# Output projection of the last token tile split between the attention steps and the tail, and a new order inside each attention step, in a two-block transformer kernel

## What is computed

```
# block 1, layers 0 and 1
mod = silu(c) @ w_ada[layer] + b_ada[layer];  shift, scale, gate = split(mod)
h = rmsnorm(x, g_pre) * (1 + scale) + shift
z = h @ w_in
layer 0: o = concat(mla_attention(8 heads), sliding_window_attention(8 heads))
layer 1: o = concat(rmsnorm((softmax(q1 k1) - lam * softmax(q2 k2)) @ v),   # 4 heads, "dif"
                    forgetting_attention(8 heads))                            # "fox"
y = (o * silu(z_gate)) @ w_out
x = x + gate * rmsnorm(y, g_post)
# block 2, layer 2
h = x @ w_in; o = concat(nsa(6 heads) * silu, stick_breaking(4 heads) * silu, hgrn2(6 heads) * silu)
x = layer_norm(ALPHA * x + o @ w_out)
```

## Time and profile before

| | |
|---|---|
| median of 3 runs (lowest, highest) | 1437.36 us (1437.13, 1442.88) |
| profiled execution | 1442.61 us |
| its span in the trace, mean granted clock | 1441.1 us, 0.926 |
| PE busy | 1264.0 us, 88% |
| DVE, ACT, POOL busy | 554.3, 427.3, 113.7 us |

### The profile page before, as it was taken

One profiled execution on the slowest core, in us unless ns is written; L12 is line 12 of the kernel. 1 busy time (PEld: TensorE's weight loads), 2 busy tenths in 40 slices (PEclk: granted clock), 3 DMA queues, 4 the chain that ended last, 5 costly groups with the idle time before them and its releaser, 6 DMA issues.

```text
span 1441.1 us, 15111 instructions
## 1 busy us (share of the span) xinstructions
PE 1264.0 (88%) x5264; PEld 699.6 (49%) x5264; DVE 554.3 (38%) x1422; ACT 427.3 (30%) x1086; POOL 113.7 (8%) x140
## 2 busy tenths in 40 slices
PE   4889986899998999889999989989998999856974
PEld 1555543445564444334455555555454545545541
DVE  3233322333544520334442432112125731667871
ACT  0133022334432201322234332114233533651211
POOL 0000000000001000000000000000000000484722
PEclk9989997999998999999999999989999999966986
DMA  9222334444000432322111004241101111000000
GB/s 349 92 81 64 112 117 172 146 175 118 1 1 1 117 59 59 52 67 58 59 59 59 1 11 131 59 161 44 45 0 45 44 59 59 1 0 31 1 30 29
DMA packets 60258, 99.71 MB, mean 69 GB/s; under 512 B 12068, under 2 KB 22129, under 8 KB 60184
## 3 DMA queue, kind: packets, MB, share of 16 engines
q1 hardware_dynamic: 54370, 93.58, 20.8%
q10 hardware_dynamic: 5814, 5.18, 1.1%
HBM read 96.60 MB, written 4.08 MB: 70 GB/s over the span
## 4 chain that ended last, share of the span: by engine, by line
PE 72%; DVE 14%; ACT 5%; issue 3%; DMA 3%; POOL 2%; ACTq 1%; DVEq 0%; SPq 0%; POOLq 0%
PE PR L856 29%; PE SC L908 6%; PE OB L886 6%; PE PT L768 6%; PE PR L768 4%; PE OB L768 4%; PE SC L768 4%; PE PT L923 3%; PE PR L949 3%; DMA ring<-in_w_ada 3%; DVE d L1661 2%; DVE stage L1661 2%; POOL arena L1569 2%; DVE tok L1661 1%; DVE arena L1877 1%
## 5 line engine op out<-in xcount | busy, mean ns | idle before, releaser
L856 PE MATMUL PR<-ring,hT 128*128 128x512 f32 (+1 forms) x784 | 381.2, 599 | 9.3 <-DVE arena L1817 6.3
L1349 ACT ACTIVATE stage<-stage,nmax 128x256 f32<-128x256 f32 (+7 forms) x200 | 103.7, 519 | 335.3 <-DVE nmax L1981 311.2
L856 PEld LDWEIGHTS PR<-ring,hT 128*128 128x128 f32 x784 | 136.3, 198 | 114.4 <-issue 98.4
L886 PEld LDWEIGHTS OB<-arena,pts 128*128 128x128 f32 (+3 forms) x880 | 132.2, 202 | 97.4 <-issue 75.9
L908 PE MATMUL SC<-arena 64*128 64x256 f32 (+15 forms) x432 | 147.5, 452 | 10.0 <-DVE nmax L1981 10.0
L856 PE MATMUL PR<-hT,ring 128*128 128x512 f32 (+1 forms) x304 | 152.8, 626 | 0.0
L1569 POOL TENSOR_TENSOR arena<-arena 128x192 f32<-128x192 f32 (+1 forms) x118 | 80.5, 683 | 826.1 <-PE OB L886 778.2
L886 PE MATMUL OB<-arena,pts 128*128 128x64 f32 (+4 forms) x880 | 131.0, 278 | 9.2 <-ACT pts L1197 9.2
L923 PEld LDWEIGHTS PT<-ident,stage 128*128 128x128 f32 (+3 forms) x440 | 58.2, 145 | 131.0 <-issue 65.1
L923 PE MATMUL PT<-ident,stage 128*128 128x128 f32 (+3 forms) x440 | 87.5, 290 | 34.7 <-ACT stage L1328 15.9
L1197 ACT ACTIVATE pts<-PT 128x256 f32<-128x256 f32 (+7 forms) x200 | 80.7, 404 | 58.4 <-issue 22.2
(11 more groups left out here) (337 smaller groups left out, 1306.6 us busy)
## 6 DMA issues: line engine op xcount, KB each, us to landing
ring<-in_w_ada SPq DMA_DIRECT2D x12, 2048.0 KB, 8.8
ring<-in_od_w_in SPq DMA_DIRECT2D x8, 2048.0 KB, 14.6
ring<-in_w_in SPq DMA_DIRECT2D x5, 1536.0 KB, 6.8
ring<-in_ev_w_in SPq DMA_DIRECT2D x3, 2048.0 KB, 7.7
ring<-in_w_in SPq DMA_DIRECT2D x3, 2048.0 KB, 9.8
ring<-in_ev_w_out SPq DMA_DIRECT2D x2, 2048.0 KB, 10.1
ring<-in_od_w_out SPq DMA_DIRECT2D x2, 2048.0 KB, 8.7
ring<-in_w_out SPq DMA_DIRECT2D x2, 2048.0 KB, 7.8
```

Source lines behind the costliest of these rows:

```text
L856: mm = pe.matmul(dst, l, r, start=(k == 0), stop=(k == KT - 1))
L886: mm = pe.matmul(ob[:, h * w:h * w + w], pts[0:rows_, v % 2, n * P:n * P + P], vb, start=(n == 0), stop=(n == len(blocks) - 1))
L1349: give(act.activation(pb[:, s % NP, 0:n], zm[:, s % 2, 0:n], ACT.Exp, bias=nmax[:, row, c:c + 1], scale=-1.0, accum_out=rsum[:, row, c:c + ...
```

## The change

1. **Output projection ahead.** Of the last tile's output projection in layers 0 and 1 (16 calls: two halves h of 8 calls over k), the 4 calls of each half whose k belongs to the first half of the mixed features become filler at the end of the attention ("ahead", 4 units each), and so does the transpose `mT` that they need. Their two groups stay open in the two filler banks; `last_tile` transposes the other half and closes them with the other 4 calls each.
2. **`SPREAD`.** To fit this, the spread of layers 0 and 1 is new. In layer 1, 14 steps carry the first 15 tiles in place of 15 steps (8 or 9 units each in place of 8).
3. **Order in a step, all layers.** DVE: `finish_gates`, weights of v, masks of the new scores, and then `finish_behind`, which does for the step **before** the late group part, the group, the chains and `tile_done` of all tiles but `mT` and `hT` ("urgent", still in their own step). ACT: exponentials, `finish_behind` of the step before, copy of the transposed weights, urgent tiles.

```diff
+AHEAD = {0: 0, 1: 0}
+def last_ahead(L):
+    return [("mT", L, T - 1, AHEAD[L])], [("ahead", L, 0), ("ahead", L, 1)]
...
-SPREAD = [[(4, 5)] + [(3, 4)] * 6 + [(5, 9), (2, 1), (4, 10), (2, 1), (2, 9), (2, 5)], [(15, 15), (4, 12), (4, 8), (2, 1), (2, 5), (2, 1), (2, 1), (2, 5)], [(21, 68), (4, 14)]]
+SPREAD = [[(4, 5)] + [(3, 4)] * 6 + [(5, 9), (2, 1), (4, 10), (2, 1), (2, 7), (2, 1), (1, 1), (2, 5)], [(15, 14), (4, 11), (1, 1), (2, 1), (2, 7), (2, 1), (2, 6), (2, 1), (2, 1), (4, 5)], [(21, 68), (4, 14)]]
...
-UNITS = {"adac": 1, "adas": 2, "adag": 1, "mT": 1, "hT": 1}
+UNITS = {"ahead": 4, "adac": 1, "adas": 2, "adag": 1, "mT": 1, "hT": 1}
+URGENT = ("mT", "hT")
+def urgent(done):
+    return [name for name in done if name[0] in URGENT]
...
+            def output_half(L, h, g):
+                i = T - 1
+                p = prn["y", L, i, h]
+                if g == AHEAD[L]:
+                    b = free_bank(p)
...
+                freed(pe, ("mT", L, i, g))
+                W = weights(("wo", L, h))
+                for k in range(4 * g, 4 * g + 4):
+                    mm = pe.matmul(b[:, :], hT[:, k, i * P:i * P + P], W[:, k, :], start=(k == 4 * AHEAD[L]),
+                                   stop=(k == 7 - 4 * AHEAD[L]))
...
+                behind = None
                 for r_, (v, (_, g, j, sus), new) in enumerate(steps(L)):
+                    done = schedule[L][1][r_] if r_ < len(schedule[L][1]) else []
+                    finish_gates()
+                    if r_:
+                        finish_weights(v, g, sus)
                     for s in new:
...
+                    if behind:
+                        finish_behind(*behind)
+                    if urgent(done):
+                        finish_gates()
+                    for name in urgent(done):
+                        tile_done(name)
+                    behind = (v, done)
+                finish_gates()
+                finish_behind(*behind)
                 finish_group(L, len(plan[L]) - 1)
```

More of the change, by code:

```diff
@@ L194, in last_tile @@
     def last_tile(L):
-        jobs.extend(finish_tile(L, T - 1))
+        jobs.append(("mT", L, T - 1, 1 - AHEAD[L]))
+        jobs.extend(("y", L, T - 1, h) for h in range(2))
         chunk_end[("wo", L, 0)] = chunk_end[("wo", L, 1)] = len(jobs)
@@ L202, in fillers @@
         for name, tiles in FILLERS[L]:
-            chunk(name, tiles)
+            chunk(name, [t for t in tiles if t[0] != "ahead"])
     jobs.append(("cols",))
@@ L327, in two_block_kernel @@
     beside |= {("gate0", 0, 0), ("gate1", 0, 0), ("gate1", 0, 1), ("nz", 0)}
+    beside |= {("y", L, T - 1, h) for L in (0, 1) for h in range(2)}
+    late_halves = {("mT", L, T - 1, 1 - AHEAD[L]) for L in (0, 1)}
     bank_of, nth, per_bank, turn = [], [], [0] * 8, [0, 0]
@@ L807, in tile_matmuls @@
                     L, i, g = name[1:]
-                    if kind == "mT" and g == 0:
+                    if kind == "mT" and i == T - 1:
+                        ahead, last = (2 * i, 2 * i + 1) if L == 0 else (i, T + i)
+                        pe.wait_ge(ob_free, g_no[L, ahead if g == AHEAD[L] else last] + 1)
+                    elif kind == "mT" and g == 0:
                         pe.wait_ge(ob_free, g_no[L, 2 * i + 1 if L == 0 else T + i] + 1)
@@ L814, in tile_matmuls @@
                     yield
+                    return
+                if kind == "ahead":
+                    yield from output_half(*name[1:], AHEAD[name[1]])
                     return
@@ L959, in last_tile @@
                     pe.wait_ge(pt_ev[r], (sum(e[0] <= L for e in v_units) + 1 - r) // 2)
-                for name in finish_tile(L, T - 1):
-                    whole_tile(name)
+                late = 1 - AHEAD[L]
+                whole_tile(("mT", L, T - 1, late))
+                for h in range(2):
+                    for _ in output_half(L, h, late):
+                        pass
                 for i in LEFT[L]:
@@ L1328, in stick_tail, with finish_behind @@
                         give(act.activation(pb[:, s % NP, 0:n], zm[:, s % 2, 0:n], ACT.Exp), p_done, s + 1)
+                def finish_behind(r_, v, done):
+                    if v >= 1 and v_units[v - 1][0] == L and last_v[L, v_units[v - 1][1]] == v - 1 \
+                            and v_units[v - 1][3][0][0] == "dif":
+                        rsqrt(DH)
+                    for chain in chains:
+                        next(chain, None)
+                    for name in done:
+                        if name[0] not in URGENT:
+                            tile_done(name)
+                        if name[0] == "hf":
+                            next(chains[-1])
+                    if L == 2 and r_ in HG_EARLY:
+                        exponentials(HG_EARLY.index(r_))
+                behind = None
                 for r_, (v, (_, g, j, sus), new) in enumerate(steps(L)):
+                    done = schedule[L][1][r_] if r_ < len(schedule[L][1]) else []
                     for s in new:
@@ L1362, in attention @@
                     give(copy(pts[0:r, v % 2, 0:w], PT[v % 2][0:r, 0:w]), pt_ev[v % 2], v // 2 + 1)
[L1363 to L1374, removed]
+                    for name in urgent(done):
+                        tile_done(name)
+                    behind = (r_, v, done)
+                finish_behind(*behind)
             def exponentials(c):
@@ L1985, in attention @@
                         stick_tail()
[L1986 to L2009, removed]
+                    if r_ == 0:
+                        finish_weights(v, g, sus)
+                    if behind:
+                        finish_behind(*behind)
+                    if urgent(done):
+                        finish_gates()
+                    for name in urgent(done):
+                        tile_done(name)
+                    behind = (v, done)
+                finish_gates()
+                finish_behind(*behind)
                 finish_group(L, len(plan[L]) - 1)
```

49 lines of the change are left out of this document (45 added, 4 removed).

## The result

The changed kernel takes 1497.32 us (median of 4 runs, 1494.61 to 1501.32) against 1440.12 us for the kernel before: a ratio of 1.0396, 95% interval 1.0352 to 1.044. It is slower by 57 us. I had forecast slower by 17, with a range that ended at 1467.

The account below looks back on a forecast made before the run. PE was taken to bound the kernel, busy for 1264.0 of 1441.1 us. Terms summed to +17.4 on the profiled 1442.61, 1460.0, or 1455 us against the runs' median of 1437.36; range 1430 to 1467, likeliest 1445 to 1466.

Parts of the forecast that it names:

- the first mechanism, the late releases: All layers: filler bank releases stand behind the next step's masks, so PE waits; likeliest case, 1445 to 1466 us, chance 0.67.
- the sum: Whole kernel: 14 + 2 + 12 + 4.8 - 9.5 - 5.4 - 0.5 = +17.4 us.
- Waits of the banks: Layer 0 gates and layer 1 dif steps: PE waits for late filler bank releases, about 40 us in all.
- Dif steps: Layer 1, steps 9 to 14 and behind ff: seven new bank waits; with clock, 28.8 us for 16.6, so +12.
- Idle PE: Layers 0 and 1: new waits, among them +14 for layer 0's gates and rows, less waits filled or ended.
- The clock: Layer 1 dif: 1.3 us each behind five long waits, 6.5 against 3.4 before; layer 0: 1.3 gained by projection ahead.
- the clock falls too: Layer 0 and fox part: each new wait followed by one half-clock call, 1.1 us each, ten times; 1466 us, chance 0.05.
- Projection ahead: End of layers 0 and 1: calls moved from the tail into attention; -5.4 us in layer 0, -0.5 in layer 1.
- Layer 2: Cmp weight waits end, -7.1 us, and ACT's order gains some 2.4; -9.5 in all, bounds -6 and -14.
- Tails: After layers 0 and 1: 8 fewer output projection calls each; -9.1 us in layer 0, -7.9 in layer 1.
- The third rival: Whole kernel, nothing measurable: losses of about half (+17) against gains of 25; 0 to +7, about 1441 us, chance 0.14.
- The second: Whole kernel, releases are in time: -25, 1412 us, or 1428 if half the releases are; chance 0.14.

Follow-up runs that it names:

- experiment 3: Changed kernel, but every filler tile released in its own step; gates, weights first and deferred groups stay: 1440.36 us, ratio 0.997.
- Experiment 9: Kernel before, with the conditioning row's copy on DVE made twice, so its bank comes free 0.7 us later: 1449.88 us, ratio 1.0045.
- experiment 1: Changed kernel with the kernel before's order inside a step on DVE and ACT; projection ahead and both new spreads stay: 1452.2 us, ratio 1.005.
- experiments 6: Changed kernel with layer 0's tiles and fv released in their own step and 15 steps of 8 units in layer 1: 1425.12 us, ratio 0.9873.
- 10: Changed kernel with the work of the step before placed ahead of masks and exponentials, not behind them: 1430.65 us, ratio 0.9908.
- 12: Kernel of experiments 6 with ff's DMAs on POOL and, in layer 2 alone, the step before's work ahead of masks and exponentials: 1420.11 us, ratio 0.9821.

## Why the prediction was wrong in size

The direction and the first mechanism, the late releases, hold; the size was off by a factor of three. The step that failed is the price of lower clock behind the new waits: +1.8 us in the sum, 27 measured. By stages the missing 39 us of the profiled execution are 22.5 in the attentions of layers 0 and 1, 7.4 in layer 2's, 5.8 in the tails, 3.9 ahead of layer 0's attention, and -0.5 at the end. By the prediction's own steps:

- **Waits of the banks: right, place by place.** Gates 1.3 to 1.5 where none was: measured 1.30, 1.37, 1.44, 1.50, and 3.05, 3.33, 3.19 where 1.91, 2.35, 2.01 stood. Dif steps 2.7, 3.1, 1.35, 0.65, 4.1, 4.8 and 5.6: measured 2.70, 3.08, 1.24, 0.52, 3.97, 5.41 and 5.24. Strip sums were to be 1.06 later at five places, 5.3 us; they are 8.0 longer at six (0.87 became 1.98).
- **Idle PE: right in the sum, by luck in layer 0.** There it grew by 13.0 us and the sum had 13.4 (13.7 + 2 - 2.3 of filled waits). But the waits for rows and strip sums grew by 16.9, and the wait for the DMA of weights at 240.49, 9.08 us before, shrank to 4.06, since PE came later to it; that wait was not in the sum. In layer 1 it grew by 12.1 where the sum had some 14 (22.3 - 13.2 + 4.8).
- **The clock: the term that failed.** For layer 0 the sum has no lower clock behind any wait ("above: +17 with a slower clock behind three of them" is only its bound), and 1.3 us of gain at the stage's end; for layer 1 it has "6.5" for five waits in the dif steps, against 3.4 before. So it had -1.3 and +3.1; measured were 15.5 and 11.3, 25 us more. That these are mostly the releases' doing is shown by experiment 3, which takes away 13.3 and 13.9 us of busy time. I priced one slow call behind a wait (1.1 us). Experiment 9 has 5.4 us of longer matmuls for three waits that are 0.7 us longer, and at its third place half clock for 9 us. The price was also read from the wrong row: the call of 2.05 us behind 1.91 us stands where the clock had been down since the wait of 9.08 us at 236.24, and it is as slow in experiment 3, with no wait ahead of it. The rival "the clock falls too" had the mechanism and 0.05 of chance, and also counted one call for each wait.
- The Trainium skill's rule on cycled PSUM banks ("TensorE: Matmul & The Clock Gate", "A second HAM failure mode: psum-queue depth-cycling") was right here, and I had weighed it against one row of 0.87 us. By that rule the waits had to be priced with the lower throughput behind them; the trace agrees, with 0.86 granted in layer 0's attention for 0.91. Not every wait does it: one of 2.70 us (712.59) left the clock up.
- **Projection ahead: wrong in layer 0.** -5.4 and -0.5 forecast, +4.7 and -0.7 measured alone (experiment 1). The forecast for layer 1 holds. In layer 0 the moved calls were to fill waits and keep the clock up; with them the last 20 us are at 0.74 of the clock, and the stage's busy time is up by 11.1 us for 7.3 of calls.
- **Layer 2: wrong.** -9.5 forecast with bounds of -6 and -14, -2.1 measured. The cmp waits went, from 7.1 to 0.5 us in this stage, and those for ACT fell from 15.9 to 7.0, more than I had. But ACT's copy out of PT now stands behind `finish_behind`, whose chains and tile work wait for DVE, and the values' waits for it grew from 5.1 to 17.0. I had called that order a gain of 2.4. ACT and PE of the changed kernel, 1197 to 1200:

```profile
1197.57 0.63 ACT L1369 ACTIVATE arena<-arena 128x512 f32<-128x512 f32 x1 [4.66 <-DVE arena L1733]
...
1198.89 0.49 ACT L1250 ACTIVATE pts<-PT 128x384 f32<-128x384 f32 x1
```

```profile
1199.53 1.51 PE L936 MATMUL OB<-arena,pts 128*128 128x64 f32 x6 [3.05 <-ACT pts L1250]
```

- **Tails:** layer 1 -6.9 against -7.9, right. After layer 0 -4.3 against -9.1; the same stage takes 128.3 to 131.8 us in the runs with the projection ahead, with granted clocks of 0.96 to 0.94, so 3 us of the difference may be chance.
- The third rival needed bank waits to absorb one another; they did not. Its terms as written, +17 against 25, also do not give its 0 to +7. The second needed releases in time; experiments 6, 10 and 12 are that case, made real by another order. Its time for half of the releases, 1428, should be 1433 by its own terms.

Open: why the clock stays low for under 4 us behind one wait and 9 behind a slightly longer one; how the loss in fv's steps divides between the release and the 14 steps; and the 3 to 4 us by which stages of identical instructions differ from run to run, which hide whether layer 0's projection ahead and POOL's DMAs pay.

## What to carry to other kernels

A buffer release must not stand behind work that waits for the engine that needs the buffer: then each release comes a fixed time after that engine's last instruction, however idle the releasing engine was. Whether this shows depends on where the next user begins in the step, so an order and a spread of filler must be judged together. And price a new short wait of TensorE with the clock behind it: here that was 27 us beside 35 of idle time (experiment 3), and 5.4 beside 1.8 (experiment 9). Before reading such a price from a slow call behind a wait, look whether the calls ahead of the wait were slow already.

## What was unexpected of the hardware

At one place a wait of 2.01 us is followed by under 4 us at half clock, and one of 2.73 us by 9 us; at another a wait of 3.08 us is followed by no more of it than one of 2.35. In the kernel with an extra copy 1.8 us of idle PE came with 5.4 us of longer matmuls; with two extra copies 4.5 with 6.5. A wait of 2.70 us in the dif steps (712.59) left the clock up, one of 3.08 us 12 us later did not. After the wait of about 9 us for weights half clock lasted, from PE's restart on, for 12 us with another wait of 1.91 us in between (before) and for 16 us with none (experiment 3): work without a wait did not bring the clock back sooner.
